# The sample sequences' SSM states in a two-layer hybrid decoder step: two alternating slots and masked sums, against unrolled quarters, three slots and column tiles

## Chip, core and metric

One core of a Trainium2 chip. The metric is the device time of one launch in microseconds: the median over the runs, smaller is better.

## What is computed

The kernel is one inference step of a decoder with an even layer (a depthwise convolution and latent attention) and an odd layer (Mamba-2 SSD), each followed by gated cross-attention. A prompt of 1024 tokens and 8 sample sequences of 4 tokens share the weights. The change touches one part of the odd layer: the carried state of the 8 sample sequences. For each sequence `b` there is a state of 32 heads x 64 x 128 numbers (1 MB in float32). From the reference, for one sequence's 4 tokens:

```python
y = y + jnp.einsum('btgn,bgepn->btgep', cf, state) * jnp.exp(cum)[..., None]
to_end = jnp.exp(cum[:, -1:] - cum) * dt
new_state = (state * jnp.exp(cum[:, -1])[..., None, None]
             + jnp.einsum('bsge,bsgn,bsgep->bgepn', to_end, bf, xf))
```

So the old state is read by the tokens' C vectors (the inter term, into YS), is scaled by a decay per head, and gets an update, a sum over 4 tokens of B times X; the new state is an output. The rest of `y` is computed later, in the chunks.

## The kernel before

The odd layer runs its stages one after the other, with a barrier of all engines between them: projections, then `ssd_all` (L2918), which loads small vectors, calls `sample_states` (L2966; the stage of this text), then `ssd_chunks` (L2623: 8 prompt chunks of 128 tokens and one chunk with the 32 sample tokens), then `store_state`. The order of the work on each engine is written out by hand, engine by engine, with semaphores.

**Data of the stage.** The state of a sequence lies as 128 partitions x 16 blocks (k) x 128, in `SB`, in two slots (sequence b in slot b % 2). `NW`, two slots, holds the new state until it is stored. All 8 PSUM banks are used: four named U and four named V, which change roles from one sequence to the next. XT holds the sample tokens' convolved x, B and C by channel, BT is B by token (32 x 512), XE is x by token scaled by to_end (32 x 2048), `bm` is a 0/1 mask of which of the 32 tokens belongs to sequence b. DE holds the decays. YS (32 x 2048) gathers the inter term.

**Head of the stage.** SyncE loads XT (L2986), eight small rows of ce (L2989) and the first two states (L2992). TensorE turns x and B of the tokens (L3019, L3021). VectorE copies BT (L3075), forms te (L3077), clears YS (L3078, 32 x 2048), and after ScalarE's exponential forms XE (L3082) and copies ce (L3086). Only then does TensorE begin with the states.

**One sequence (b).**
- TensorE: 16 transposes of the state (L3028) into the four banks of slot b; 4 matmuls of 128 x 32 by 128 x 512 (L3036), one per group, C against the turned state, each into the partitions 0 to 31 of a bank of the other side (all 32 tokens, of which 4 are of sequence b); 16 matmuls (L3041) with 32 rows that multiply the masked x by B, into the four banks from which the turned state has been copied; then the transposes of b + 1.
- ScalarE: copies the turned state from the four banks to SBT (L3067), one slot.
- VectorE: masks XE by sequence (XM, L3089, 32 x 2048), scales the state by the decay (L3091, 128 x 2048), adds the masked rows of the four banks to YS (L3097, four of 32 x 512), adds update and scaled state into NW (L3107, four of 128 x 512).
- SyncE: when VectorE is done with b - 2's state, it issues the load of state b (L2997), and for b = 2 to 5 one of four 2 MB parts of the output weights WO (L3001).
- GpSimd: issues the store of NW (L3011). VectorE waits for the store two sequences back (f_s) before it writes that NW slot.

These follow one another through semaphores: L3036 waits for all four copies (f_te) and the previous sequence's NW (f_un); the transposes of b + 1 wait for YS (f_yo). GpSimd waits for all stores at the end of the stage.

**The next stage.** `ssd_chunks` issues on SyncE's queue the loads of XT (L2662, 1.5 MB), CBt (L2666, 2 MB) and Z (L2670). TensorE's first instruction (L2713) waits for XT; VectorE's (L2841) for CBt. Before the first chunk's inter matmuls TensorE waits for WO (r_w 64, L2726), though WO is first used in `out` of chunk 0 (L2702), which runs in chunk 1.

Of the kernel before, what the change touches and what calls it, by code (L numbers as in the profile page):

```python
# [22 lines left out]
P = 128  # L23
# [105 lines left out]
def build(nc, A, O):  # L129
# [2493 lines left out]
    def ssd_chunks(W, DTt, CUt, ST, YS):  # L2623
# [6 lines left out]
        with ExitStack() as c:  # L2630
# [63 lines left out]
            def _(pe):  # L2694
                def out(n, T, halves=(0, 1)):

                    for hf in halves:
                        if hf == 0:

                            pe.wait_ge(r_ye, n * 4 + 4)  # L2700
                        for k in range(NX):
                            m = nc.tensor.matmul(OP[hf][0:T, :], YT[:, k, 0:T], WO[:, k, hf * 512:(hf + 1) * 512],  # L2702
                                                 start=k == 0, stop=k == NX - 1)
                        m.then_inc(r_om, 1)

                def chunk(n, T, sample, first):
# [206 lines left out]
    f_l = [sem(f"state_slot{k}") for k in range(2)]  # L2913
    f_s = [sem(f"state_stored{k}") for k in range(2)]
    f_tp, f_te, f_yi, f_yo, f_xm, f_up, f_un, f_out, f_c = (sem(n) for n in (
        "fs_tp", "fs_tp_out", "fs_inter", "fs_inter_out", "fs_xm", "fs_update", "fs_new", "fs_stored", "fs_x_loaded"))
# [23 lines left out]
    def store_state(ST):  # L2940

        with ExitStack() as c:
# [10 lines left out]
            @block.vector  # L2953
            def _(dve):
                dve.wait_ge(f_tp, NB + 2)
# [10 lines left out]
    def sample_states(DTt, CUt, DE, msk, bm, YS, WO):  # L2966

        with ExitStack() as c:
            XT = sb(c, "fXT", [P, XB, SMP])
            XE, BT = sb(c, "fXE", [SMP, SI]), sb(c, "fBT", [SMP, 4, SN])  # L2970
            XM = [sb(c, f"fXM{a}", [SMP, SI]) for a in range(2)]
            SB = [sb(c, f"fSB{a}", [P, NX, SN]) for a in range(2)]
            NW = [sb(c, f"fNW{a}", [P, NX, SN]) for a in range(2)]
            SBT = sb(c, "fSBT", [P, SI])
            ce, te = sb(c, "fce", [SMP, SH]), sb(c, "fte", [SMP, SH])
            U = [pb(c, f"fU{a}") for a in range(4)]
            V = [pb(c, f"fV{a}") for a in range(4)]
            BK = (U, V)
# [6 lines left out]
            def _(sp):  # L2985
                sp.dma_start(XT[:], xbc_d[:, :, TP:TOK].rearrange("n p t -> p n t")).then_inc(f_c, 16)  # L2986

# [6 lines left out]
                for b in range(2, NB):  # L2994

                    sp.wait_ge(f_un, 1 + b - 1)
                    sp.dma_start(SB[b % 2][:], s_in[b]).then_inc(f_l[b % 2], 16)  # L2997
                    if b < 6:

                        part = slice(4 * (b - 2), 4 * (b - 1))  # L3000
                        sp.dma_start(WO[:, part, :], w_out[:, part, :]).then_inc(r_w, 16)  # L3001

            @block.gpsimd
            def _(pool):

                for count in (f_yi, f_yo, f_up, f_un):
                    pool.nop().then_inc(count, 1)
                with loop(pool, 0, NB // 2) as j:
                    for s in range(2):
                        pool.wait_ge(f_un, 1 + 2 * j + s + 1)  # L3010
                        pool.dma_start(s_out[bass.ds(2 * j + s, 1)].rearrange("b p k n -> p (b k) n"), NW[s][:]).then_inc(f_s[s], 16)  # L3011
# [4 lines left out]
            def _(pe):  # L3016
                pe.wait_ge(f_c, 16 * (NB + 1))
                for k in range(NX):
                    nc.tensor.transpose(U[k // 4][0:SMP, (k % 4) * P:(k % 4 + 1) * P], XT[:, k, :], ident[:])  # L3019
                for g in range(4):  # L3020
                    t = nc.tensor.transpose(V[0][0:SMP, g * P:(g + 1) * P], XT[:, NX + g, :], ident[:])  # L3021
                t.then_inc(f_tp, 1)
                pe.wait_ge(dve_own.sem, d0 + 6)
                def turn(b, s, step):

                    pe.wait_ge(f_l[s], 16 * (step + 1))
                    for k in range(NX):
                        t = nc.tensor.transpose(BK[s][k // 4][:, (k % 4) * P:(k % 4 + 1) * P], SB[s][:, k, :], ident[:])  # L3028
                    t.then_inc(f_tp, 1)

                def batch(b, s, step, last=False):

                    pe.wait_ge(f_te, 4 * b + 4)
                    pe.wait_ge(f_un, 1 + b)
                    for g in range(4):
                        m = nc.tensor.matmul(BK[1 - s][g][0:SMP, :], XT[:, NX + 4 + g, :], SBT[:, g * 512:(g + 1) * 512],  # L3036
                                             start=True, stop=True)
                    m.then_inc(f_yi, 1)
                    pe.wait_ge(f_xm, b + 1)
                    for k in range(NX):  # L3040
                        m = nc.tensor.matmul(BK[s][k // 4][:, (k % 4) * P:(k % 4 + 1) * P], XM[s][:, k * P:(k + 1) * P],  # L3041
                                             BT[:, k // 4, :], start=True, stop=True)
                    m.then_inc(f_up, 1)
                    if not last:

                        pe.wait_ge(f_yo, 1 + b + 1)
                        turn(b + 1, 1 - s, step + s)

                turn(0, 0, 0)
                with loop(pe, 0, NB // 2 - 1) as j:  # L3050
                    for s in range(2):
                        batch(2 * j + s, s, j)
                batch(NB - 2, 0, NB // 2 - 1)
                batch(NB - 1, 1, NB // 2 - 1, True)

            @block.scalar
            def _(act):
                act.wait_ge(dve_own.sem, d0 + 3)
                nc.scalar.activation(te[:], te[:], ACT.Exp).then_inc(act_own.sem, 1)
                with loop(act, 0, NB // 2) as j:  # L3060
                    for s in range(2):
                        b = 2 * j + s
                        act.wait_ge(f_tp, b + 2)

                        act.wait_ge(f_yi, 1 + b)
                        for g in range(4):
                            nc.scalar.activation(SBT[:, g * 512:(g + 1) * 512], BK[s][g][:], ACT.Copy).then_inc(f_te, 1)  # L3067

# [3 lines left out]
            def _(dve):  # L3072
                v, N = (lambda ins: dve_own.step(dve, ins)), nc.vector
                dve.wait_ge(f_tp, 1)
                v(N.tensor_copy(BT[:], V[0][0:SMP, :].rearrange("p (g n) -> p g n", g=4)))  # L3075
                dve.wait_ge(f_c, 16 * (NB + 1))
                v(N.tensor_tensor(te[:], ce[:], CUt[0:SMP, NQ, :], ALU.subtract))  # L3077
                v(N.memset(YS[:], 0.0))  # L3078
                dve.wait_ge(act_own.sem, a0 + 1)
                v(N.tensor_tensor(te[:], te[:], DTt[0:SMP, NQ, :], ALU.mult))  # L3080
                for g in range(4):
                    dve_own_ins = N.tensor_tensor(XE[:, g * 512:(g + 1) * 512].rearrange("p (h e) -> p h e", e=SP_),  # L3082
                                                  U[g][0:SMP, :].rearrange("p (h e) -> p h e", e=SP_),
                                                  te[:, g * 8:(g + 1) * 8].unsqueeze(2).to_broadcast([SMP, 8, SP_]), ALU.mult)
                v(dve_own_ins)
                v(N.tensor_copy(ce[:], te[:]))  # L3086
                def ready(b, s):

                    N.tensor_scalar(XM[s][:], XE[:], bm[:, bass.ds(b, 1)], None, ALU.mult).then_inc(f_xm, 1)  # L3089
                    dve.wait_ge(f_tp, b + 2)  # L3090
                    v(N.tensor_tensor(SB[s][:], SB[s][:], DE[:, :, bass.ds(b, 1)].to_broadcast([P, NX, SN]), ALU.mult))  # L3091

                def batch(b, s, step, last=False):
                    dve.wait_ge(f_yi, 1 + b + 1)
                    for g in range(4):
                        part = YS[:, g * 512:(g + 1) * 512]
                        ins = N.scalar_tensor_tensor(out=part, in0=BK[1 - s][g][0:SMP, :], scalar=bm[:, bass.ds(b, 1)],  # L3097
                                                     in1=part, op0=ALU.mult, op1=ALU.add)
                    ins.then_inc(f_yo, 1)
                    dve.wait_ge(f_yo, 1 + b + 1)  # L3100
                    dve.wait_ge(f_up, 1 + b + 1)
                    if not (isinstance(step, int) and step == 0):

                        dve.wait_ge(f_s[s], 16 * step)
                    for g in range(4):
                        part = slice(4 * g, 4 * g + 4)
                        ins = N.tensor_tensor(NW[s][:, part, :], SB[s][:, part, :],  # L3107
                                              BK[s][g][:].rearrange("p (k n) -> p k n", k=4), ALU.add)
                    ins.then_inc(f_un, 1)
                    if not last:  # L3110
                        ready(b + 1, 1 - s)

                ready(0, 0)
                batch(0, 0, 0)
                batch(1, 1, 0)
                with loop(dve, 1, NB // 2 - 1) as j:
                    dve_own.enter(j - 1, 2)
                    for s in range(2):
# [40 lines left out]
```

## Time and profile of the kernel before

| what | us |
|---|---|
| median of 3 runs | 3184.64 (3182.26 to 3197.51) |
| the profiled execution, own time | 3189.32 |
| its span in the profile | 3187.7 |
| `sample_states`, from the first load's issue (L2986) to the next stage's first issue (L2662) | 2013.25 to 2147.17: 133.9 |
| one sequence in the middle of it | 13.1 |

The profile is one execution taken by the hardware profiler. PE is TensorE's matmuls, PEld its weight loads, DVE is VectorE, ACT ScalarE, POOL GpSimd, SPq and POOLq the queues on which SyncE and GpSimd issue transfers. Times are in microseconds from the start of the span. Over the whole span TensorE is busy 88%, VectorE 47%, ScalarE 24%, GpSimd 16%. PEclk is the clock that TensorE was granted, as a share of full speed. A float32 matmul shows as two records, a transpose as one. In a timeline row, what stands in brackets is the engine's idle time before it and what ended it.

### The profile page before, as it was taken

To read this page: it belongs to the slowest core of one execution; us is meant where nothing else is said; L and a number is where in the kernel's file an instruction comes from. 1 tells how busy PE (TensorE), PEld (TensorE's weight loads), DVE (VectorE), ACT (ScalarE), POOL (GpSimd) and SP (SyncE) were. 2 spreads that over 40 slices of the span, in tenths; PEclk is the share of its full clock that TensorE was granted. 3 is DMA by queue.
4 is the path that set the end of the run, shared out by engine and by line. 5 is a ranking of instruction groups with operands and counts; after the bars stand their busy time and mean duration, and the time that the engine had idled before them with its cause. 6 is when DMAs were issued, how large, how long until landed. Compare 5 with 4: busy or idle time off the path is not lost. (4 is left out here: it accounts for less than half of the span.)

```text
span 3187.7 us, 40235 instructions
## 1 busy us (share of the span) xinstructions
PE 2791.4 (88%) x16311; PEld 2213.6 (69%) x16311; DVE 1485.6 (47%) x2481; ACT 767.1 (24%) x1451; POOL 520.1 (16%) x422
## 2 busy tenths in 40 slices
PE   5999896897978999898998699667999995899889
PEld 4998564675856997778998477445555543599676
DVE  4997664564321005445655400356777733100453
ACT  3221353232211212323222211112222111121231
POOL 1012000341301210121221010002121211121011
PEclk9999898997988998998999899787999897899999
DMA  3211001761031114203221221464332303211431
GB/s 98 60 38 45 14 1 70 277 241 61 1 119 53 47 56 170 80 1 85 87 92 62 80 95 47 137 209 118 108 99 79 74 1 114 65 47 40 168 110 48
DMA packets 235495, 270.70 MB, mean 85 GB/s; under 512 B 36358, under 2 KB 190534, under 8 KB 230099
## 3 DMA queue, kind: packets, MB, share of 16 engines
q1 hardware_dynamic: 215506, 179.83, 18.9%
q0 software_dynamic: 16384, 75.77, 6.6%
q10 hardware_dynamic: 3456, 12.98, 1.0%
q8 instruction: 110, 1.80, 0.2%
q14 instruction: 39, 0.32, 0.0%
HBM read 226.64 MB, written 41.28 MB: 84 GB/s over the span
## 5 line engine op out<-in xcount | busy, mean ns | idle before, releaser
L306 PE MATMUL pp<-HH,WS_part 128*128 128x352 f32 x1776 | 574.9, 324 | 0.0
L304 PE MATMUL pp<-HH,WH 128*128 128x352 f32 x1344 | 436.9, 325 | 40.1 <-POOL WS_part L443 40.1
L305 PE MATMUL pp<-HT_part,WH 128*128 128x352 f32 x1344 | 435.0, 324 | 0.0
L306 PEld LDWEIGHTS pp<-HH,WS_part 128*128 128x128 f32 x1776 | 337.2, 190 | 0.0
L304 PEld LDWEIGHTS pp<-HH,WH 128*128 128x128 f32 x1344 | 254.8, 190 | 42.1 <-POOL WS_part L443 42.1
L2702 PE MATMUL OP<-oWO,YT 128*128 128x512 f32 (+1 forms) x576 | 255.8, 603 | 3.3 <-DVE XE L2829 3.3
L305 PEld LDWEIGHTS pp<-HT_part,WH 128*128 128x128 f32 x1344 | 254.9, 190 | 0.0
L2161 DVE COPY HT<-zT 128x512 f32<-128x512 f32 x64 | 44.2, 691 | 437.1 <-DMA xown<-c_batch 383.6
L443 POOL TENSOR_TENSOR WS_part<-WS,WH 128x1024 fp32r<-128x1024 f32 x56 | 140.4, 2507 | 655.0 <-ACT WH L394 655.0
L2702 PEld LDWEIGHTS OP<-oWO,YT 128*128 128x128 f32 (+1 forms) x576 | 104.8, 183 | 146.4 <-issue 142.9
L998 DVE SCALAR_TENSOR_TENSOR CV<-GXP,cw,CV 128x512 f32<-128x512 f32 x240 | 161.9, 739 | 0.0
L304 PE MATMUL pp<-HH,CK_part 128*128 128x352 f32 x432 | 142.0, 329 | 7.9 <-DVE HT_part L863 7.9
L305 PE MATMUL pp<-HT_part,CK_part 128*128 128x352 f32 x432 | 140.5, 325 | 0.0
L304 PE MATMUL zp<-WZH,HH 128*128 128x512 f32 (+1 forms) x288 | 114.6, 398 | 14.7 <-ACT ZS L2540 14.0
L304 PE MATMUL yp<-QT_part,KM_part 128*128 128x512 f32 (+1 forms) x288 | 115.0, 399 | 13.2 <-DVE WO_part L606 13.2
L306 PE MATMUL yp<-QT_part,SGX_part 128*128 128x512 f32 (+1 forms) x288 | 114.8, 399 | 0.0
L305 PE MATMUL yp<-WO_part,KM_part 128*128 128x512 f32 (+1 forms) x288 | 114.7, 398 | 0.0
L306 PE MATMUL zp<-WZH,HT_part 128*128 128x512 f32 (+1 forms) x288 | 113.8, 395 | 0.0
L305 PE MATMUL zp<-WZ_part,HH 128*128 128x512 f32 (+1 forms) x288 | 113.5, 394 | 0.0
L2683 POOL TENSOR_TENSOR XK<-XK,Db 128x2048 f32<-128x2048 f32 (+1 forms) x9 | 88.1, 9786 | 136.8 <-DVE XD L2855 136.8
L2382 DVE SCALAR_TENSOR_TENSOR oACC<-EP,cwo,oACC 128x1024 f32<-128x1024 f32 x72 | 98.7, 1370 | 9.2 <-DVE oACC L2380 2.4
L1732 DVE COPY QN<-KTp 128x512 f32<-128x512 f32 x128 | 82.7, 686 | 27.6 <-PE KTp L1658 27.6
(493 smaller groups left out, 5224.6 us busy)
## 6 DMA issues: line engine op xcount, KB each, us to landing
WS<-x_w_qg SPq DMA_DIRECT2D x32, 512.0 KB, 4.0
WO<-cache_mem_k SPq DMA_DIRECT2D x16, 1024.0 KB, 4.9
WO<-cache_mem_v POOLq DMA_DIRECT2D x16, 1024.0 KB, 5.4
CBt<-cum_scratch SPq DMA_DIRECT2D x8, 2048.0 KB, 10.1
xbc_scratch<-oACC ACTq DMA_DIRECT2D x24, 528.0 KB, 2.7
WS<-o_w_in SPq DMA_DIRECT2D x24, 512.0 KB, 3.7
XT<-xbc_scratch SPq DMA_DIRECT2D x8, 1536.0 KB, 7.5
WS<-e_w_in SPq DMA_DIRECT2D x18, 512.0 KB, 3.9
```

The lines of the kernel that those rows point to most:

```text
L304: nc.tensor.matmul(out, wh, xh, start=start, stop=False)
L305: nc.tensor.matmul(out, wh, xl, start=False, stop=False)
L306: return nc.tensor.matmul(out, wl, xh, start=False, stop=stop)
L443: nc.gpsimd.tensor_tensor(WL[:, k % slots, :, :], WS[:, k % slots, :, :], WH[k % 2][:, :, :], ALU.subtract).then_inc(p_lo, 1)
L998: ins = nc.vector.scalar_tensor_tensor(out=out, in0=src, scalar=tap, in1=out, op0=ALU.mult, op1=ALU.add)
L1732: nc.vector.tensor_copy(KTs[:, r, :], KTp[r % 3][:]).then_inc(d_kte, 1)
L2161: nc.vector.tensor_copy(KBT[b % 2][:, 2 * q:2 * q + 2, :], KTp[:].rearrange("p (k m) -> p k m", k=2))\
L2382: ins = nc.vector.scalar_tensor_tensor(out=out, in0=src, scalar=tap, in1=out, op0=ALU.mult, op1=ALU.add)
L2683: nc.gpsimd.tensor_tensor(XK[R, :].rearrange("p (h e) -> p h e", h=SH), XK[R, :].rearrange("p (h e) -> p h e", h=SH), Db[R, :].unsqueeze(2 ...
L2702: m = nc.tensor.matmul(OP[hf][0:T, :], YT[:, k, 0:T], WO[:, k, hf * 512:(hf + 1) * 512], start=k == 0, stop=k == NX - 1)
```

## The change

The loop over sequences is unrolled on every engine. Each sequence is cut in quarters of 4 blocks. PSUM is divided anew: three banks for turned quarters (TPp), four for updates (UP), one (ACC) for the inter term. The state gets three slots, SBT two. TensorE's order becomes: for each quarter q, transposes of quarter q of b + 1 (`turn`), update matmuls of quarter q of b (`update`), and after quarter 0 the inter matmuls of b (`inter`). In `inter` the four groups go to four column tiles, partitions 32g to 32g + 31 of one bank, which keeps summing over all 8 sequences; the C operand CMB is masked so that other tokens add zero. The mask for the update moves from x (32 x 2048) to B (BM, 32 x 512). VectorE forms the new state in one operation per block, state x decay + update (16 of 128 x 128), with no separate scaling pass and no YS sums. After the last sequence ACC is copied, and four matmuls with column slices of the identity bring the four partition groups to partitions 0 to 31, from where they are copied to YS. The four WO parts are issued after all state loads, and the wait for them moves from the first chunk to `out`.

```diff
@@ ssd_chunks, TensorE: out, chunk
                             pe.wait_ge(r_ye, n * 4 + 4)
+                            pe.wait_ge(r_w, 64)
...
-                    if first:
-                        pe.wait_ge(r_w, 64)
-                    else:
+                    if not first:
@@ sample_states, SyncE
-                for s in range(2):
-                    sp.dma_start(SB[s][:], s_in[s]).then_inc(f_l[s], 16)
+                for b in range(NB):
+                    if b >= 3:
+                        sp.wait_ge(f_un, 4 * (b - 2))
+                    sp.dma_start(SB[b % 3][:], s_in[b]).then_inc(f_l[b % 3], 16)
...
+                for a in range(4):
+                    sp.dma_start(WO[:, 4 * a:4 * a + 4, :], w_out[:, 4 * a:4 * a + 4, :]).then_inc(r_w, 16)
@@ GpSimd
+                for b in range(NB):
+                    pool.wait_ge(f_un, 4 * (b + 1))
+                    pool.dma_start(s_out[b], NW[b % 2][:]).then_inc(f_s[b % 2], 16)
@@ TensorE
+                def turn(b, q):
+                    if q == 0:
+                        pe.wait_ge(f_l[b % 3], 16 * (b // 3 + 1))
+                    i = 4 * b + q
+                    if i >= 3:
+                        pe.wait_ge(f_te, i - 2)
+                    for k in range(4):
+                        t = nc.tensor.transpose(TPp[i % 3][:, k * P:(k + 1) * P], SB[b % 3][:, 4 * q + k, :], ident[:])
+                    t.then_inc(f_tp, 1)
+                def inter(b):
+                    pe.wait_ge(f_te, 4 * b + 4)
+                    for g in range(4):
+                        m = nc.tensor.matmul(ACC[32 * g:32 * g + 32, :], CMB[:, g, b, :], SBT[b % 2][:, g * 512:(g + 1) * 512],
+                                             start=b == 0, stop=b == NB - 1, tile_position=(0, 32 * g), skip_group_check=True)
+                    m.then_inc(f_yi, 1)
+                def update(b, q):
+                    if q == 0:
+                        pe.wait_ge(f_xm, b + 1)
+                    i = 4 * b + q
+                    if i >= 4:
+                        pe.wait_ge(f_un, i - 3)
+                    for k in range(4):
+                        m = nc.tensor.matmul(UP[q][:, k * P:(k + 1) * P], XE[:, (4 * q + k) * P:(4 * q + k + 1) * P],
+                                             BM[b % 2][:, q, :], start=True, stop=True)
+                    m.then_inc(f_up, 1)
...
+                for q in range(4):
+                    turn(0, q)
+                pe.wait_ge(dve_own.sem, d0 + 7)
+                for b in range(NB):
+                    for q in range(4):
+                        if b + 1 < NB:
+                            turn(b + 1, q)
+                        update(b, q)
+                        if q == 0:
+                            inter(b)
+                pe.wait_ge(f_un, 4 * NB + 1)
+                for g in range(4):
+                    m = nc.tensor.matmul(UP[g][0:SMP, :], ident[:, 32 * g:32 * g + 32], YA[:], start=True, stop=True)
+                m.then_inc(f_up, 1)
@@ ScalarE
+                        nc.scalar.activation(SBT[b % 2][:, q * 512:(q + 1) * 512], TPp[i % 3][:], ACT.Copy).then_inc(f_te, 1)
@@ VectorE
+                v(N.memset(CMB[:], 0.0))
...
+                for b in range(NB):
+                    ins = N.tensor_copy(CMB[:, :, b, TS * b:TS * b + TS], XT[:, NX + 4:NX + 8, TS * b:TS * b + TS])
...
-                v(N.memset(YS[:], 0.0))
...
+                def masked(b):
+                    if b >= 2:
+                        dve.wait_ge(f_up, 4 * (b - 1))
+                    N.tensor_scalar(BM[b % 2][:], BT[:], bm[:, b:b + 1], None, ALU.mult).then_inc(f_xm, 1)
...
+                for b in range(NB):
+                    if b + 1 < NB:
+                        masked(b + 1)
+                    if b >= 2:
+                        dve.wait_ge(f_s[b % 2], 16 * (b // 2))
+                    for q in range(4):
+                        dve.wait_ge(f_up, 4 * b + q + 1)
+                        for k in range(4 * q, 4 * q + 4):
+                            ins = N.scalar_tensor_tensor(out=NW[b % 2][:, k, :], in0=SB[b % 3][:, k, :], scalar=DE[:, k, b:b + 1],
+                                                         in1=UP[q][:, (k - 4 * q) * P:(k - 4 * q + 1) * P], op0=ALU.mult, op1=ALU.add)
+                        ins.then_inc(f_un, 1)
+                dve.wait_ge(f_yi, NB)
+                N.tensor_copy(YA[:], ACC[:]).then_inc(f_un, 1)
+                dve.wait_ge(f_up, 4 * NB + 1)
+                for g in range(4):
+                    ins = N.tensor_copy(YS[:, g * 512:(g + 1) * 512], UP[g][0:SMP, :])
+                v(ins)
```

## Rows read from the trace of the kernel before

**Rows 1.** The windows view, first two rounds; columns on its first line.
```profile
core 0: us, PE busy (x) PEld busy (x) DVE busy (x) ACT busy (x) POOL busy (x), PEclk, DMA share, GB/s
2030.70:2045.40 14.70, 12.33 (x57) 7.99 (x57) 6.28 (x6) 2.07 (x4) 0.00 (x0) 0.70 0.01 1
2045.40:2058.50 13.10, 10.95 (x57) 6.39 (x56) 8.58 (x10) 2.06 (x4) 1.24 (x1) 0.87 0.68 228
```

**Rows 2.** The timeline, stage's start and second round: start, us, engine, line, what.
```profile
2018.62 2.76 SPq L2992 DMA_DIRECT2D fSB<-state_ssm  x2
...
2025.67 1.76 DVE L3078 MEMSET YS<- 32x2048 f32 x1 [0.48 <-DVE fte L3077]
...
2030.75 3.68 PE L3028 MATMUL fU<-ident,fSB 128*128 128x128 f32 x16 [6.49 <-DVE fce L3086]
...
2047.37 2.06 ACT L3067 ACTIVATE fSBT<-fV 128x512 f32<-128x512 f32 x4 [10.76 <-PE fV L3028]
...
2048.10 0.69 SPq L2997 DMA_DIRECT2D fSB<-state_ssm  x1
...
2049.49 5.32 PE L3036 MATMUL fU<-fSBT,fXT 128*32 128x512 f32 x8 [2.15 <-ACT fSBT L3067]
...
2054.74 3.64 PEld L3041 LDWEIGHTS fV<-fBT,fXM 32*128 32x128 f32 x32 [0.84 <-issue]
2054.74 3.83 PE L3041 MATMUL fV<-fBT,fXM 32*128 32x128 f32 x32
2054.92 2.71 DVE L3097 SCALAR_TENSOR_TENSOR YS<-fU,bm,YS 32x512 f32<-32x512 f32 x4 [3.50 <-PE fU L3036]
...
2058.50 1.96 PE L3028 MATMUL fU<-ident,fSB 128*128 128x128 f32 x16
2058.68 2.48 DVE L3107 TENSOR_TENSOR fNW<-fSB,fV 128x512 f32<-128x512 f32 x4 [1.05 <-PE fV L3041]
```

**Rows 3.** The timeline at the stage's end and the next's start.
```profile
2137.01 2.48 DVE L3107 TENSOR_TENSOR fNW<-fSB,fV 128x512 f32<-128x512 f32 x4 [1.90 <-issue]
2140.41 1.15 POOL L3011 DMA_DIRECT2D out<-fNW  x1 [12.96 <-DVE fNW L3107]
2147.17 0.37 SPq L2662 DMA_DIRECT2D XT<-xbc_scratch  x1
...
2154.77 3.67 PE L2713 MATMUL V<-ident,XT 128*128 128x128 f32 x16 [17.85 <-DMA XT<-xbc_scratch]
...
2162.00 0.20 DVE L2841 COPY dc<-CBt 128x32 f32<-128x32 f32 x1 [14.41 <-DMA CBt<-cum_scratch]
```

**Rows 4.** The groups by line and form on VectorE: mean ns of one.
```profile
L878 DVE SCALAR_TENSOR_TENSOR CKV<-pe,krs,X_part 128x128 f32<-128x128 f32 x8 | 2.8, 346 | 1.8 <-POOL krs L1012 1.8
...
L2324 DVE COPY HC<-ohp 128x24 f32<-128x24 f32 x24 | 2.2, 171 | 9.7 <-PE ohp L2312 9.7
```

**Rows 5.** The timeline on TensorE, even layer's sample attention, scores in column tiles.
```profile
640.77 1.04 PE L1671 MATMUL Sc<-QN,DTt_part 128*32 128x512 f32 x8
641.75 1.53 PE L1658 MATMUL KTp<-ident,HT 128*128 128x128 f32 x12
```

**Rows 6.** The timeline on TensorE, the round where L3036 ran at full clock.
```profile
2089.20 3.62 PE L3036 MATMUL fV<-fSBT,fXT 128*32 128x512 f32 x8 [2.31 <-ACT fSBT L3067]
```

**Rows 7.** The instructions of tile fSB: landing times of its loads.
```profile
DMA to landing us min/median/max: 6.3/6.5/8.6
```

**Rows 8.** The DMA view, window 2048 to 2060: two queues, one landing.
```profile
q1 hardware_dynamic: 899, 2.57, 63.4%
q0 software_dynamic: 272, 1.05, 23.1%
...
out<-fNW POOLq DMA_DIRECT2D x1, 1024.0 KB, 10.0
```

**Rows 9.** The DMA view, window 2018 to 2030, the row of queue q1.
```profile
q1 hardware_dynamic: 1458, 2.10, 66.0%
```

**Rows 10.** The DMA view, window 2126 to 2138, the row of queue q0.
```profile
q0 software_dynamic: 272, 1.05, 30.1%
```

More of the change, by code:

```diff
@@ L2912, in build @@
     r_seg = sem("ssd_seg_ready")
[L2913 removed]
+    f_l = [sem(f"state_slot{k}") for k in range(3)]
     f_s = [sem(f"state_stored{k}") for k in range(2)]
[L2915 to L2916 removed]
+    f_xt, f_tp, f_te, f_yi, f_xm, f_up, f_un, f_out, f_c = (sem(n) for n in (
+        "fs_x_tp", "fs_tp", "fs_tp_out", "fs_inter", "fs_masked", "fs_update", "fs_new", "fs_stored", "fs_x_loaded"))
     def ssd_all(DTt, CUt, DE):
@@ L2968, in sample_states @@
         with ExitStack() as c:
-            XT = sb(c, "fXT", [P, XB, SMP])
+            XT, CMB = sb(c, "fXT", [P, XB, SMP]), sb(c, "fCMB", [P, 4, NB, SMP])
             XE, BT = sb(c, "fXE", [SMP, SI]), sb(c, "fBT", [SMP, 4, SN])
-            XM = [sb(c, f"fXM{a}", [SMP, SI]) for a in range(2)]
-            SB = [sb(c, f"fSB{a}", [P, NX, SN]) for a in range(2)]
+            BM = [sb(c, f"fBM{a}", [SMP, 4, SN]) for a in range(2)]
+            SB = [sb(c, f"fSB{a}", [P, NX, SN]) for a in range(3)]
             NW = [sb(c, f"fNW{a}", [P, NX, SN]) for a in range(2)]
[L2974 to L2978, printed above, removed]
+            SBT = [sb(c, f"fSBT{a}", [P, SI]) for a in range(2)]
+            ce, te, YA = sb(c, "fce", [SMP, SH]), sb(c, "fte", [SMP, SH]), sb(c, "fYA", [P, 512])
+            TPp = [pb(c, f"fTP{a}") for a in range(3)]
+            UP = [pb(c, f"fUP{a}") for a in range(4)]
+            ACC = pb(c, "fACC")
             s_in = A["state_ssm"][0].rearrange("b (k a) p n -> b (a p) k n", a=2)
@@ L3024, in turn @@
[L3024 to L3054, printed above, removed]
+                    t = nc.tensor.transpose(ACC[0:SMP, g * P:(g + 1) * P], XT[:, NX + g, :], ident[:])
+                t.then_inc(f_xt, 1)
+                for q in range(4):
+                    turn(0, q)
+                pe.wait_ge(dve_own.sem, d0 + 7)
@@ L3056, in _ @@
             @block.scalar
             def _(act):
-                act.wait_ge(dve_own.sem, d0 + 3)
+                act.wait_ge(dve_own.sem, d0 + 4)
                 nc.scalar.activation(te[:], te[:], ACT.Exp).then_inc(act_own.sem, 1)
[L3060 to L3067, printed above, removed]
+                for b in range(NB):
+                    for q in range(4):
+                        i = 4 * b + q
+                        act.wait_ge(f_tp, i + 1)
+                        if q == 0 and b >= 2:
+                            act.wait_ge(f_yi, b - 1)
+                        nc.scalar.activation(SBT[b % 2][:, q * 512:(q + 1) * 512], TPp[i % 3][:], ACT.Copy).then_inc(f_te, 1)
@@ L3086, in _ @@
+                v(ins)
                 v(N.tensor_copy(ce[:], te[:]))
[L3087 to L3118, printed above, removed]
-                        batch(2 * j + s, s, j)
-                    dve_own.leave(NB // 2 - 2)
-                batch(NB - 2, 0, NB // 2 - 1)
-                batch(NB - 1, 1, NB // 2 - 1, True)
+                def masked(b):
+                    if b >= 2:
+                        dve.wait_ge(f_up, 4 * (b - 1))
+                    N.tensor_scalar(BM[b % 2][:], BT[:], bm[:, b:b + 1], None, ALU.mult).then_inc(f_xm, 1)
@@ new lines, in _ @@
+                masked(0)
+                for b in range(NB):
+                    if b + 1 < NB:
+                        masked(b + 1)
+                    if b >= 2:
+                        dve.wait_ge(f_s[b % 2], 16 * (b // 2))
+                    for q in range(4):
+                        dve.wait_ge(f_up, 4 * b + q + 1)
[3 more added lines that the diff above has]
+                        ins.then_inc(f_un, 1)
```

31 lines of the change are left out of this document (8 added, 23 removed).

## The prediction

> **What bounds the kernel now.** I read the windows view over the stage first [rows 1]. A round, one sample sequence, takes 13.1 us, and in it no engine is full: TensorE 10.95, VectorE 8.58, ScalarE 2.06. So the round is a chain of waits. The timeline shows it [rows 2]: transposes of the next state (1.96 us), ScalarE's copies (2.06) with TensorE idle 2.15 before the inter matmuls, these (5.32), the update matmuls (3.83), and transposes again. VectorE's sums and additions hang beside it. The sum 1.96 + 2.15 + 5.32 + 3.83 is 13.3, less small overlaps the 13.1. Eight rounds and a head and tail make the stage's 133.9 us, and a barrier stands at either end. At its end [rows 3] VectorE finishes at 2139.5, the last store is issued at 2140.41, and the next stage issues its load of XT at 2147.17. TensorE starts there when XT lands (2154.77), VectorE when CBt does (2162.00). What follows is untouched, so the whole change is worth what those two landings move.
>
> **The change, part by part.** I lay out a new timeline against the profiled execution (3189.32 us, span 3187.7); that one lies 4.7 us, 0.15%, above the median, so I subtract the same gain from 3184.64.
>
> *VectorE.* Scaling, masked x and YS sums go. Per sequence there are 16 operations of 128 x 128 with a PSUM operand. The nearest row has 346 ns for one [rows 4]; four of 32 x 512 of the same operation end in 2.71 us, so one starts before the other ends by about 0.07, and I take 0.276 each: 4.4 us, plus a mask of 32 x 512 at about 0.4. That is 4.8 us in place of 8.58, off the path. Its last quarter ends about 1.2 us after TensorE's.
>
> *TensorE.* Transposes as before, 16 for 1.97 less the pipeline's end: 1.8. Updates as before: 3.8. The inter matmuls in four column tiles: the same form stands in the even layer, where eight records of 128 x 512 take 1.04 us and the next group starts 0.98 after them [rows 5], against 3.62 us one behind the other at full clock [rows 6] and 5.32 with a clock that fell. I take 1.0. The work is 6.6 us. The Trainium skill, page "TensorE: Matmul & The Clock Gate", section "Measured speedup vs the span model", has 2.38 times for three column tiles; by that the inter part would be some 1.5 us and a round 0.5 longer. Row 640.77 is this form with four tiles and gives 3.5 times, so I go by the row.
>
> *Switches between forms.* The new order mixes 128-row transposes, 32-row updates and column tiles: nine switches per sequence where there were three. From updates to transposes the matmuls go on without a gap (3.83 from 2054.74, next at 2058.50) [rows 2]; before a switch to updates the weight loads stand still for 0.84. Neither is the cost in the new order: the lower bound is 0, the upper 0.84. A drained pipeline must pay the latency that a transpose shows beyond its slot, some 0.2 us (1.96 for 16 that start every 0.11), and that is the nearest: 9 x 0.2 = 1.8. So TensorE needs 8.4 us a round (6.6 with free switches, 14.2 with the dearest).
>
> *ScalarE* has the same 2.06 us in quarters [rows 2], with three banks ahead of it: hidden behind TensorE's updates; without that cover up to 2.15 us a round come back.
>
> *The load loop.* SyncE waits for VectorE's end of b - 3, issues 0.1 to 0.2 us later, and the state lands 6.3 to 8.6, median 6.5 us, after the issue [rows 7]. TensorE wants it one own round later. So a round can't be under 1.2 + 0.2 + 6.5 + 0.1 = 8.0 us, or 10.1 with a landing of 8.6. *The store loop.* VectorE waits for the store of b - 2: about 1 us to issue, 10.0 to land beside WO [rows 8], then its own 4.8; two rounds hold this if one is 7.9. *Transfers.* A load of 1.05 MB costs half of 66.0% of 12 us, 4.0 us of the DMA engines [rows 9]; a store 23.1% of 12, 2.8, to 30.1% of 12, 3.6 [rows 8, 10]: 6.8 to 7.6 a round. All these lie just under 8.4; I take **8.4 us a round**, 4.7 less than now.
>
> *Head.* The YS memset (1.76 us) leaves VectorE's chain [rows 2]; eight copies of at most 0.17 each come in [rows 4], the CMB memset runs while it waits. The start at 2030.75 becomes about 2030.1. The first state's transposes (3.68 us at half clock) move into the wait, as the first load, issued at 2018.62, lands after 6.3 or a little more, near 2025. Round 0 began with a granted clock of 0.70 [rows 1]; I give it 11.5 us, between 8.4 and about 15.
>
> *Sum.* Round 0 ends at 2041.6, six rounds of 8.4 at 2092.0, round 7, without transposes, at 2097.1, VectorE's last state at 2098.3. New tail: copy of ACC 0.7, four matmuls one behind the other 5.3 (3.6 at full clock), four copies to YS 2.5 (as L3107): 2107. The last store, issued at 2099.3 and landing in 10.0 us instead of 6.1, ends at 2109.3; it decides. Next stage's issue: 0.6 later, **2109.9** against 2147.17.
>
> *What is late next: WO.* Its four parts, 8.4 MB, are now issued behind the last state load, when VectorE ends sequence 4 (2041.6 + 33.6 + 1.2 = 2076.4), on the queue that carries XT, CBt and Z afterwards. In window 2048 to 2060 q1 moves 2.57 MB in 63.4% of 12, 7.6 us; less the state's 4.0, 1.52 MB of WO take 3.6, so 8.4 MB take 20 us. With one load (4.0) and four stores (11.2 to 14.4) that is 35 to 38 us from about 2077.5 on: until some 2114.5. XT's 1.5 MB come behind it; alone it lands 7.6 us after its issue, some 5.5 of it transfer. XT then lands near **2120**, not 2117.5, and CBt, on the same queue, keeps its distance. Gain: 2154.8 - 2120, about 35 us. The wait for WO, moved to `out`, is met long before and costs nothing. Predicted: 3184.6 - 35 = **3150 us**; the profiled time would be 3154.
>
> **Rivals.**
> 1. *Forecast*, 0.72: rounds of 7.6 to 9.5 us. The lower end, a clock that rises at once and no WO ahead of XT give 3140; the upper 3156.
> 2. *The load loop rules*, 0.08: landings of 8.6 as the longest one, a round of 10.1. Stage end 2109.9 + 6 x 1.7 = 2120, XT 2127.7: gain 27, 3158. For it: each load now runs beside a store from the start; against: the loads already do so in rows 7, and land in 6.5.
> 3. *The change doesn't do what it says*: the column tiles run one behind the other, 0.08. The inter part is then 3.6 us, the round 11.0, the stage's end 2128, XT at 2135.7: gain 19, 3166. Against it stands row 640.77.
> 4. *The clock stays at its lower level*, 0.08, because TensorE keeps stopping in small waits. Twice the 6.6 and 1.8 for switches: 15 us a round. The stage's end moves to about 2158, XT to 2166: 11 us slower than now, 3196, within 0.5%. Against: in the second round the clock was 0.87 with 2.15 us of idle in it, and the new order has less idle.
> 5. *Slower: the switches*, 0.04. Each of nine costs the 0.84 that rows 2 show before L3041, and these stops hold the clock down: 13.2 + 7.6 = 21 us a round. Stage end near 2200, XT 2208: 54 us slower, 3238. It decides from 13.4 us a round on, and is slower by 0.5% from 15.5. The Trainium skill, page "TensorEngine Tiling (Array Packing)", section "Key Properties", speaks for it: a change of tiling mode drains the engine. The trace agrees that something stands still (0.84), but the updates' first matmul starts at 2054.74, before the inter matmuls' last one ends (2049.49 + 5.32), so TensorE itself loses little there.
>
> **Numbers.** A measurement of this kernel can tell some 0.5%, 16 us, from no change. Faster by more: cases 1, 2, 3, 0.88. Within: case 4, 0.08. Slower: 0.04. The range 3135 to 3168 holds cases 1 to 3 with the bounds of the switches (free ones make 8.0 the round, the load loop's; 10.5 makes 3160).
>
> **What would show it.** Right: rounds of 8 to 9 us between first transposes of successive states, TensorE over 85% busy in them and PEclk near 1; inter groups of about 1 us; VectorE idle a third of a round; load landings near 6.5; the next stage's XT issued at about 2110 and landing over 8 us later, with WO still moving. Wrong: rounds over 11 us; a PEclk of 0.5 to 0.7 in the middle rounds; VectorE waiting for a store (f_s); inter groups of 3.6 us; or XT landing in 7.6 us, which would say that WO is out of the way by then.

## The result

The median of the changed kernel is 3168.72 us against 3189.55 before, in nine runs each. One run of the nine took 6950.69 us and is set aside as disturbed; the median of the other eight is 3167.96. The ratio without it is 0.9946, 95% interval 0.9923 to 0.997. The two medians lie 21 us apart, the ratio stands for 17: about 0.5 to 0.7%, where 35 us were forecast, and at the upper end of the range (3135 to 3168). The others spread from 3161.60 to 3187.01 where the kernel before spreads from 3182.26 to 3197.51. The profiled execution took 3163.62 us.

The windows view of the changed kernel, over five of its rounds (columns in its first line):

```profile
core 0: us, PE busy (x) PEld busy (x) DVE busy (x) ACT busy (x) POOL busy (x), PEclk, DMA share, GB/s
2025.20:2032.90 7.70, 7.70 (x57) 5.71 (x57) 4.20 (x14) 2.50 (x5) 0.00 (x0) 1.00 0.27 77
2032.90:2040.60 7.70, 7.70 (x57) 5.66 (x56) 4.87 (x17) 2.39 (x4) 1.21 (x1) 1.00 0.61 173
2041.60:2055.70 14.10, 14.10 (x58) 10.19 (x57) 4.90 (x18) 2.39 (x4) 1.15 (x1) 0.50 0.57 177
2055.70:2069.70 14.00, 14.00 (x57) 10.14 (x56) 4.82 (x18) 2.39 (x4) 1.15 (x1) 0.50 0.49 150
2092.40:2100.00 7.60, 7.60 (x57) 5.64 (x56) 4.79 (x18) 2.39 (x4) 1.15 (x1) 1.00 1.02 411
```

These answer to [rows 1]. A round now takes 7.7 us at a granted clock of 1.00 and 14.1 at 0.50, the lower of TensorE's two levels (1.2 and 2.4 GHz). TensorE is busy all through in both. The clock was at the upper level for two rounds, at the lower from 2041 to 2089, and up again after that.

The timeline of the changed kernel on TensorE, where the clock falls (start, duration, what; the idle time before and its releaser in brackets):

```profile
2038.88 0.66 PE L3016 MATMUL fTP<-ident,fSB 128*128 128x128 f32 x4
...
2041.03 0.66 PE L3016 MATMUL fTP<-ident,fSB 128*128 128x128 f32 x4 [0.41 <-DMA fSB<-state_ssm]
...
2041.62 2.07 PE L3034 MATMUL fUP<-fBM,fXE 32*128 32x128 f32 x8
...
2043.62 1.94 PE L3022 MATMUL fACC<-fSBT,fCMB 128*32 128x512 f32 x8
```

Up to 2041 TensorE has not stopped for 15 us. Then it waits 0.41 us for the load of the fourth state, and the next group already runs at half speed (2.07 in place of 1.15, then 1.94 in place of 1.07). The timeline at the stage's end answers to [rows 3]:

```profile
2106.05 4.22 DVE L3111 SCALAR_TENSOR_TENSOR fNW<-fSB,DE,fUP 128x128 f32<-128x128 f32 x16 [3.71 <-DMA out<-fNW]
2110.19 0.68 DVE L3115 COPY fYA<-fACC 128x512 f32<-128x512 f32 x1
2110.83 1.15 POOL L3002 DMA_DIRECT2D out<-fNW  x1 [7.04 <-DVE fNW L3111]
...
2117.42 2.47 DVE L3118 COPY YS<-fUP 32x512 f32<-32x512 f32 x4 [6.54 <-PE fUP L3057]
2121.93 0.37 SPq L2662 DMA_DIRECT2D XT<-xbc_scratch  x1
...
2129.81 3.67 PE L2714 MATMUL V<-ident,XT 128*128 128x128 f32 x16 [12.44 <-DMA XT<-xbc_scratch]
...
2137.05 0.19 DVE L2840 COPY dc<-CBt 128x32 f32<-128x32 f32 x1 [14.69 <-DMA CBt<-cum_scratch]
```

The stage's first load is issued at 2009.19 here, so it takes 112.7 us against 133.9: 21.2 us less, as much as the medians differ. (This profile reached the stage 4 us earlier than the one before, which the change has no part in. In all 16 profiles of this text, what lies outside the stage takes 3042 to 3060 us. So a stage is compared more sharply than a total, and a few us of a median are not assigned to a cause.) XT lands 7.9 us after its issue (7.6 before), so WO hardly delayed it. But VectorE waits 3.71 us for a store at the last state.

### The profile page after: what moved, and what is told of

The parts are those of the page before. It is cut to its first block and busy times, and to the rows that moved or that the text cites. A ratio compares the mean times of both kernels' runs of the same rounds, so it can differ in the third digit from the quotient of the medians.

```text
span 3161.8 us, 40215 instructions
## 1 busy us (share of the span) xinstructions
PE 2785.7 (88%) x16319; PEld 2218.8 (70%) x16319; DVE 1458.5 (46%) x2550; ACT 769.3 (24%) x1451; POOL 518.9 (16%) x422
```

## The experiments

The theories after this result: A, this mix of transposes and of matmuls that fill 32 rows or 32 columns doesn't hold the upper clock; B, the wait for a load lets it fall. "Stage" is from the first load's issue to the next stage's first issue, in each run's profile; ratios are to the kernel before, measured beside each run (its medians are 3181 to 3192 us).

**The changed kernel again**, twice (no edit).

> The changed kernel again, for a second look at when TensorE's granted clock falls. In its first profile rounds took 7.7 us while the clock was at its upper level (first two and last rounds) and 14.06 us in between, at the lower level. Theory A (the mix of transposes and of matmuls that fill only 32 rows or 32 columns of the array does not count for much, so the clock falls although TensorE never stops): it falls again, at much the same place, and 3 to 4 rounds take 14 us; stage 105 to 115 us, 15 to 28 us faster than the kernel before. Theory B (the wait of 0.4 us for the load of the fourth state, at 2041, lets the clock fall): it falls wherever a load is waited for, so the place and the length can differ from the first profile.

> The changed kernel once more, for its spread on this chip beside the others, and a third profile of the clock. Theory C (a stop with 32-row updates lets the clock fall): some runs stop and fall, at the first load waited for, and the time then depends on how long the clock stays down: a spread of 20 us and more between runs, where four slots spread over 6. In the profile the fall comes right behind a wait for a load.

Measured: 3162.98 us (four runs, 3145.77 to 3174.88), ratio 0.9891 (0.9847 to 0.9934), stage 120.0; and 3169.25 us (twelve runs, 3149.35 to 3183.11 without one disturbed), ratio 0.9929 (0.9902 to 0.9957), stage 114.6. TensorE's timeline of the first:

```profile
2036.76 1.15 PE L3034 MATMUL fUP<-fBM,fXE 32*128 32x128 f32 x8
2038.09 0.66 PE L3016 MATMUL fTP<-ident,fSB 128*128 128x128 f32 x4 [0.18 <-DMA fSB<-state_ssm]
2038.68 1.65 PE L3034 MATMUL fUP<-fBM,fXE 32*128 32x128 f32 x8
2040.26 1.94 PE L3022 MATMUL fACC<-fSBT,fCMB 128*32 128x512 f32 x8
```

and of the second:

```profile
2038.36 1.15 PE L3034 MATMUL fUP<-fBM,fXE 32*128 32x128 f32 x8
2039.82 0.66 PE L3016 MATMUL fTP<-ident,fSB 128*128 128x128 f32 x4 [0.31 <-DMA fSB<-state_ssm]
2040.41 2.01 PE L3034 MATMUL fUP<-fBM,fXE 32*128 32x128 f32 x8
```

In all three profiles the clock falls at the first wait for a load, after two rounds of 7.7 us: 0.41, 0.18 and 0.31 us of waiting. It stayed down for 3.4, over 5 and 4.4 rounds; the stages of 112.7, 120.0 and 114.6 us follow that order. The first of these expectations gave A 105 to 115, which 120.0 misses.

**No later loads.** `for b in range(NB)` becomes `for b in range(3)` in SyncE's loads, and `turn` waits for `f_l[b % 3], 16`; loads 4 to 8 are left out. WO is still issued when VectorE ends the fifth sequence (`sp.wait_ge(f_un, 20)`).

> Only the first three states are loaded, and the slots are used again for the others; so loads 4 to 8 are left out of the computation, and TensorE never waits for one after the first rounds. Theory A: the clock falls all the same, and rounds of 14 us appear; stage 105 to 115 us, as the changed kernel. Theory B: no wait, so the clock stays at the upper level, rounds of 7.7 us to the end (the store loop may make them 8); stage about 91 us, some 43 us faster than the kernel before.

Measured: 3144.15 us, ratio 0.9844 (0.9818 to 0.9869); stage 91.2. Two windows:

```profile
2060.00:2076.00 16.00, 16.00 (x120) 12.02 (x119) 8.26 (x30) 4.91 (x9) 2.30 (x2) 1.00 0.81 294
2076.00:2085.00 9.00, 8.21 (x40) 6.05 (x38) 6.35 (x25) 0.00 (x0) 1.15 (x1) 0.54 1.02 409
```

From 2022 to 2076, seven rounds of 7.7, the clock is at 1.00. That is B's number, and A is out for these rounds: the same mix held the clock for 54 us. It isn't out for the last round, which has no transposes. There the clock falls at about 2076.6 with no stop before it, and the inter matmuls with the last twelve update matmuls take 7.4 us, where they take 3.9 in the first profile of the changed kernel, at the upper clock. The same fall without a stop stands in the last round of five more profiles with 32-row updates below (fourth slot, one column tile, one stop with 32 rows, WO late, first turn late).

**Updates over 128 rows.**

```diff
-            XE, BT = sb(c, "fXE", [SMP, SI]), sb(c, "fBT", [SMP, 4, SN])
-            BM = [sb(c, f"fBM{a}", [SMP, 4, SN]) for a in range(2)]
+            XE, BT = sb(c, "fXE", [P, SI]), sb(c, "fBT", [SMP, 4, SN])
+            BM = [sb(c, f"fBM{a}", [P, 4, SN]) for a in range(2)]
...
+                N.memset(XE[:], 0.0)
+                N.memset(BM[0][:], 0.0)
+                v(N.memset(BM[1][:], 0.0))
```

> The update matmuls take 128 rows instead of 32, of which 96 are zeros in both operands; nothing else changes, and at the same clock they should take the same time. Theory A: with whole rows in the updates the clock holds; rounds of about 7.7 us (8.0 where a load is waited for), stage about 91 to 94 us, some 40 us faster than the kernel before and 20 faster than the changed one. If zeros do not count as activity, it falls as before. Theory B: the loads are waited for as before, the clock falls as before, stage 105 to 115 us.

Measured: 3141.23 us, ratio 0.9828 (0.9809 to 0.9847); stage 89.7. Its timeline on TensorE:

```profile
2037.57 1.06 PE L3034 MATMUL fUP<-fBM,fXE 128*128 128x128 f32 x8
2038.46 0.60 PE L3016 MATMUL fTP<-ident,fSB 128*128 128x128 f32 x4
2038.90 1.06 PE L3034 MATMUL fUP<-fBM,fXE 128*128 128x128 f32 x8
2041.52 0.66 PE L3016 MATMUL fTP<-ident,fSB 128*128 128x128 f32 x4 [1.57 <-DMA fSB<-state_ssm]
2042.02 1.06 PE L3034 MATMUL fUP<-fBM,fXE 128*128 128x128 f32 x8
2043.00 1.07 PE L3022 MATMUL fACC<-fSBT,fCMB 128*32 128x512 f32 x8
```

Now TensorE stops for 1.57 us, longer than in any round of the changed kernel, and goes on at full speed. So B alone is out too. It holds through stops of 1.10 and 2.25 us as well, but not through the last one:

```profile
2070.63 1.06 PE L3034 MATMUL fUP<-fBM,fXE 128*128 128x128 f32 x8
2073.92 1.11 PE L3016 MATMUL fTP<-ident,fSB 128*128 128x128 f32 x4 [2.23 <-DMA fSB<-state_ssm]
2074.83 1.92 PE L3034 MATMUL fUP<-fBM,fXE 128*128 128x128 f32 x8
2077.93 0.66 PE L3016 MATMUL fTP<-ident,fSB 128*128 128x128 f32 x4
```

Behind 2.23 us the clock is at its lower level too, but by 2078 it is up again. With 128 rows a stop can let the clock fall; what is different is that it is back within about 4 us. The run also prices the switches: a quarter starts every 1.33 us in place of 1.67, and the two switches in it are what went, 0.17 us each. Rounds still average 7.8 us, since loads (7.2 us in all) and stores (12.9) are waited for.

**Transposes as plain matmuls.** `nc.tensor.transpose(..., ident[:])` becomes `nc.tensor.matmul(..., ident[:], start=True, stop=True)` in `turn`.

> The transposes of the states become plain float32 matmuls against the identity, two records each: 1.9 us more TensorE work a round at the upper clock, 3.8 at the lower. Theory A, if it is the transposes that do not count: the clock holds, rounds of 9.6 us, no wait for loads, stage about 103 us, 9 us faster than the changed kernel. Theory A, if it is the 32-row updates: the clock falls, rounds of 17 to 18 us, slower than the changed kernel by 10 us or more. Theory B: rounds of 9.6 leave no wait for a load, so the clock holds too.

Measured: 3159.51 us, ratio 0.9912 (0.9876 to 0.9947); stage 102.8, rounds of 9.7, no load waited for, clock 1.00. It stands with B, and with theory C, which the later expectations use: a stop lets the clock fall, and with 32-row updates it stays down for rounds.

**A fourth slot**, in ST's memory: `SB = [...three...] + [ST as 16 blocks]`, `b % 4`, load b waits for `f_un, 4 * (b - 3)`, and GpSimd clears ST behind the last transposes.

> The changed kernel with a fourth state slot (in the memory of ST, which is cleared again behind the stage), so that every load has two rounds instead of one and TensorE has no load to wait for; all loads and stores are made. After the first four runs theory C is: a stop of TensorE is what lets the clock fall, and with 32-row updates it does not come back for four to five rounds; without a stop, or with whole rows, it holds. Theory C: rounds of 7.7 to 7.9 us throughout, stage 90 to 93 us, 3140 to 3150 us in total. Rival D (the clock held without the loads because the transfers were gone, not the wait): it falls, stage 110 to 120 us.

Measured: 3140.21 us (3137.45 to 3143.28), ratio 0.9861 (0.9834 to 0.9888); stage 90.4. Two of its windows:

```profile
2021.00:2029.00 8.00, 8.00 (x60) 5.93 (x59) 4.42 (x16) 2.51 (x5) 0.00 (x0) 1.00 0.68 188
...
2061.00:2069.00 8.00, 8.00 (x64) 5.70 (x56) 4.70 (x17) 2.39 (x4) 1.47 (x2) 1.00 1.02 408
```

All transfers are made, up to 408 GB/s, and the clock holds until the last round: it was the wait, not the traffic. Rival D (the transfers) is out.

**One column tile**: `inter` writes `ACC[0:32, :]` for all four groups without `tile_position`; the inter term is not separated by group. VectorE clears ACC first.

> The four inter matmuls of a sequence all go to the first column tile, one behind the other, into partitions 0 to 31 of the bank (so the inter term is summed over groups and is not separated; that part of the result is left out). This prices the column tiles and makes a round longer than a load. At the upper clock the inter part takes 3.6 us instead of 1.07, a round 10.3. Theory C: no load is waited for, the clock holds, seven rounds of 10.3, stage 108 to 111 us: no slower than the changed kernel in its usual state (113 and 120 us). Rival (the clock falls by itself with these forms): rounds of 19 us, stage over 140 us.

Measured: 3161.45 us, ratio 0.9929 (0.9901 to 0.9956); stage 109.9, rounds of 10.2, the inter part 3.62 us. Column tiles save 2.55 us a round, 19 in the stage (91.2 with three loads). But the changed kernel, which has them, is no faster (112.7 to 120.0): the shorter round is what makes TensorE wait for a load. At the head of this run stands a stop with 32-row updates that cost little:

```profile
2021.13 0.66 PE L3016 MATMUL fTP<-ident,fSB 128*128 128x128 f32 x4 [1.11 <-DVE fce L3094]
2022.80 5.32 PE L3022 MATMUL fACC<-fSBT,fCMB 128*32 128x512 f32 x8
```

The inter matmuls take 5.32 us in place of 3.62, the clock is 0.50 from 2024 to 2026, and 1.00 from 2028 on.

**One stop added** (TensorE waits until VectorE has ended the second state) to the kernel with three loads, with 32 and with 128 rows: `if q == 0 and b == 3: pe.wait_ge(f_un, 8)` in `turn`.

> The kernel with only three loads (loads 4 to 8 left out), in which the clock held, with one stop added: before the transposes of the fourth state TensorE waits until VectorE has finished the second one, about 1.2 us. Theory C: the clock falls behind this one stop and stays at its lower level for several rounds of 14 us; stage 110 to 120 us. Rival D: one stop costs 1.2 us and no more, stage about 92 to 93 us.

> The run with one added stop of 1.3 us (three loads only; loads 4 to 8 left out), now with updates over 128 rows. Theory C: the same stop, but the clock holds, as it held through stops of 1 to 2 us with 128 rows and all loads; stage 82 to 88 us. Rival (it was the place of the stop, not the form of the work): the clock falls as it did with 32 rows, stage 100 us or more.

With 32 rows, TensorE's timeline:

```profile
2035.91 1.15 PE L3034 MATMUL fUP<-fBM,fXE 32*128 32x128 f32 x8
2038.33 0.81 PE L3016 MATMUL fTP<-ident,fSB 128*128 128x128 f32 x4 [1.26 <-issue]
2039.06 2.07 PE L3034 MATMUL fUP<-fBM,fXE 32*128 32x128 f32 x8
2041.06 1.94 PE L3022 MATMUL fACC<-fSBT,fCMB 128*32 128x512 f32 x8
```

and with 128:

```profile
2029.38 1.06 PE L3034 MATMUL fUP<-fBM,fXE 128*128 128x128 f32 x8
2031.70 0.63 PE L3016 MATMUL fTP<-ident,fSB 128*128 128x128 f32 x4 [1.26 <-issue]
2032.16 1.06 PE L3034 MATMUL fUP<-fBM,fXE 128*128 128x128 f32 x8
2033.15 1.06 PE L3022 MATMUL fACC<-fSBT,fCMB 128*32 128x512 f32 x8
```

The same stop of 1.26 us costs 16.3 us of stage in the one (107.5 against 91.2; 3151.82 us in total, 3138.93 to 3153.98) and no fall behind it in the other (stage 85.8; 3132.42 us, 3129.16 to 3134.84). The first was expected at 110 to 120. This is the plainest pair for C: the stop with 32-row updates is followed by 34 us at the lower level. (Its fastest run, 3138.93 us, has no profile; whether the clock was down as long there isn't known.) The run with 128 rows shows more:

```profile
2017.16 0.66 PE L3016 MATMUL fTP<-ident,fSB 128*128 128x128 f32 x4 [1.86 <-DVE fce L3096]
2066.65 1.48 PE L3034 MATMUL fUP<-fBM,fXE 128*128 128x128 f32 x8 [2.43 <-DVE fNW L3114]
```

The clock held through the first of these; behind the second it was at 0.50 from 2068 to 2070, and at 1.00 by 2072.

**Better versions.** Both parts; then the tail of the inter term on ScalarE and in the free transpose banks; then WO issued behind the next stage's first loads; then all four. Last, four slots with `turn(0, q)` put behind the wait for ce.

> Updates over 128 rows (96 of zeros) and the fourth slot together. TensorE's own work was 6.5 us a round in the run with 128 rows, which waited 7.2 us in total for loads and had VectorE wait 12.9 us for stores. Without the load waits: the store loop (10 us to land, 1 to issue, 4.6 of VectorE, in two rounds) gives 7.8 us a round, so about the same stage as with three slots, 88 to 90 us; if the stores land sooner than that, 82 to 86. Total 3130 to 3142 us.

> Four slots as before, and the end of the inter term moved: ScalarE copies the bank of sums as soon as the last inter matmuls are done, TensorE turns it into the free transpose banks, ScalarE writes YS; VectorE has no part in it. With four slots alone this tail lay behind VectorE's last state: copy 0.7, matmuls 5.7, copies 2.5, and the next stage's first issue came at 10.9 us behind that last state (2083.8 to 2094.7). Theory: then the last store decides, some 10 us after VectorE's end too (10.3 landing and 0.6 to issue), so the gain is 0 to 1 us: no difference that a measurement shows against four slots alone; stage 89 to 91 us, total 3138 to 3145. Rival (the tail decides): stage 84 to 86.

> As the one before, with the four WO loads issued behind the first chunk's loads of the next stage instead of inside this one. My forecast had WO delay the stores and XT. Theory: without WO beside them the last stores land in 6 to 7 us instead of 10.3, VectorE stops waiting for them, and the stage ends 4 to 8 us earlier (82 to 86 us); XT lands 7.6 us after its issue; WO is needed only about 45 us later, so nothing is paid for it. Total some 5 us below the kernel before it in this list. Rival: the stores are slow because of the state loads beside them, and the stage keeps its length.

> Updates over 128 rows, four slots, the early tail and the late WO together. With four slots and 32 rows (the two kernels with the early tail) the runs still spread over 40 and 50 us, and their profiles show a stop of 1.86 us at the head of the stage, behind the first state's transposes, in which the clock, already risen, fell. Theory C: with 128 rows no such stop lets it fall, so the spread is under 15 us and the median the lowest of all that give the whole result, 3128 to 3138; stage 82 to 87 us. Rival: the spread comes from elsewhere in the kernel and stays at 40 us.

> Four slots with 32 rows (the run that held its clock), with the first state's transposes put behind the wait for ce, as in the kernel before, so that no stop lies between them and the first round. It starts with its transposes 3.7 us later at the lower clock. Theory C: no stop anywhere in the rounds, so all runs hold the clock: median 3142 to 3148, spread under 15 us, stage 92 to 95 us. Rival: the clock also falls without a stop in some runs: spread of 30 us or more.

| kernel | updates' rows | slots | median, us (runs) | lowest to highest | ratio, 95% | stage |
|---|---|---|---|---|---|---|
| both parts | 128 | 4 | 3139.20 (4) | 3128.69 to 3147.75 | 0.9809 to 0.9879 | 87.7 |
| early tail | 32 | 4 | 3140.14 (6) | 3132.20 to 3173.07 | 0.9819 to 0.9905 | 110.5 |
| and WO late | 32 | 4 | 3143.26 (6) | 3128.41 to 3178.32 | 0.9827 to 0.9897 | 88.0 |
| all four | 128 | 4 | 3127.09 (5) | 3124.34 to 3136.88 | 0.9797 to 0.9841 | 77.9 |
| first turn late | 32 | 4 | 3141.37 (5) | 3136.29 to 3145.45 | 0.9844 to 0.9891 | 93.4 |

The two with the early tail and 32 rows missed their expectation: they spread by 41 and 50 us, and the stages are 110.5 (89 to 91 expected) and 88.0 (82 to 86). In the first one's timeline the fall stands at the head of the stage:

```profile
2011.48 0.66 PE L3019 MATMUL fTP<-ident,fSB 128*128 128x128 f32 x4 [0.37 <-ACT fSBT L3074]
2014.00 0.66 PE L3019 MATMUL fTP<-ident,fSB 128*128 128x128 f32 x4 [1.86 <-DVE fce L3102]
2014.58 1.15 PE L3037 MATMUL fUP<-fBM,fXE 32*128 32x128 f32 x8
2015.67 1.31 PE L3025 MATMUL fACC<-fSBT,fCMB 128*32 128x512 f32 x8
```

Here the clock had risen under the first transposes (0.66 for four, where the other runs have 1.1), and the wait for ce, 1.86 us, became a stop at the upper level; from 2016 to 2020 the clock is 0.54 in the mean, and three rounds took 13.4 to 14.1. But the second one has the same stop, and the same 32 rows:

```profile
2022.86 0.66 PE L3020 MATMUL fTP<-ident,fSB 128*128 128x128 f32 x4 [1.86 <-DVE fce L3103]
2024.75 1.94 PE L3026 MATMUL fACC<-fSBT,fCMB 128*32 128x512 f32 x8
2027.66 1.15 PE L3038 MATMUL fUP<-fBM,fXE 32*128 32x128 f32 x8
```

There the clock falls too, but is up again before 2028. So C doesn't say how long the clock stays down, and nothing here shows what decides it. With the first transposes behind that wait (last row) the spread is 9 us, but that kernel has the old tail, and with the old tail and the old head the fourth slot alone spread by 6: the last row doesn't show that the head made the difference. With all four parts the spread is 13.

WO late left the first four stores, beside the state loads, as slow as ever (9.2 to 10.0 us to land) and took the last four from 10.1 to 10.9 us (WO beside them) to 6.0. In the kernel with all four, VectorE ends at 2079.4, and the next stage issues at 2086.71, the last store landed. Median and stage are better than expected (3128 to 3138, 82 to 87). Its ratio, 0.9819, is the lowest of all that give the whole result, 54 us below the kernel before (3181.39 beside it), but its interval overlaps that of 128 rows alone (0.9828, 0.9809 to 0.9847); what shows the gain over that one is the stage, 77.9 against 89.7. How much of it is the late WO and how much the tail was not separated. The fourth slot adds little to the 128 rows (87.7 against 89.7), as VectorE then waits 16.2 us in all for stores.

## Why the prediction was wrong

- **The bound** and the way in which the gain comes were right: the two landings moved with the stage's end and nothing after it changed.
- **VectorE**: 16 operations in 4.2 us (forecast 4.4). It was off the path but for the last state, where the store two sequences back landed only 11.1 us after its issue, beside WO. VectorE ended 4.3 us behind TensorE there, not 1.2: the store loop, taken for harmless at 7.9 us a round, cost 3 us.
- **Inter in column tiles**: 1.07 us (forecast 1.0), by the row of the even layer [rows 5]. The Trainium skill's 2.38 times for three tiles ("TensorE: Matmul & The Clock Gate", section "Measured speedup vs the span model") was the worse guide: 3.62 against 1.07 is 3.4 times for four.
- **Switches**: 0.17 us for one (forecast 0.2). The round is 7.7 us at the upper clock, not 8.4: without switches it would be 6.3 (four quarters of 1.33 and 1.0 for the inter matmuls; forecast 6.6), so that the nine make 1.4 (forecast 1.8). Rival 5 is out, as its price of 0.84 is five times what was measured. By the Trainium skill's rule on mode changes ("TensorEngine Tiling (Array Packing)", section "Key Properties") the engine drains at one; the 0.17 us agree that something is paid.
- **The load loop**: landings of 6.7 us (median; 6.5 forecast), TensorE waits 0.2 to 0.4 us at the fourth state, a round of about 8. The forecast had this number, 8.0, and took it for harmless as it lay under 8.4.
- **The failed step** is "six rounds of 8.4": it takes the upper clock for granted. Behind the first wait for a load the clock was at its lower level for about 3.4 rounds of 14.06 us in the profile, and this is 3.4 x 6.4 = 22 us lost. The six rounds of 7.7 in place of 8.4 gave 4 of it back, round 0 another 4, the head 1; the store at the last state took 3. That makes 16, and the stage was forecast at 96.7 us and measured 112.7 (120.0 and 114.6 in the other two profiles). Rival 4, priced at 15 us a round for all rounds and given 0.08, named the mechanism, but not its trigger, and spoke against itself with "the new order has less idle": less idle did not help, as a single short stop was enough.
- **Head**: round 0 took 7.7 us, not 11.5: the clock rose at about 2024.7, at the end of the first state's transposes, which had been moved ahead.
- **Tail**: 11.7 us from VectorE's last state to the next issue, 11.6 forecast; the last store decides, as forecast (10.4 us to land). But the path by the sum's end is only 1.3 us shorter, as its four matmuls took 6.4 us at the lower clock, not 5.3.
- **WO behind the states**: the 2.5 us of delay for XT were put in and did not come: XT landed 7.9 us after its issue. Nor did they come in the kernels with a fourth slot and WO in the stage (7.6 and 7.9), which issue WO earlier. Only in the run with three slots and 128 rows, where WO was still moving when XT was issued, did XT take 9.1 us. What WO did delay were the stores (10.4 to 11.1 us beside it).

## What to carry to other kernels

When a change makes TensorE's rounds shorter, look for the first wait that it will newly meet, and price the clock behind that wait, not only the wait: here waits of 0.2 to 0.4 us were followed by 48 to 77 us at the lower level, which by the rounds of 14.06 and 7.7 us is 22 to 35 us lost. A round of nearly continuous work with 32-row matmuls in it is the fragile case here. One more buffer took the stops away; zero rows up to 128, at the same duration, let the clock hold through most stops and come back soon after the others. A wide spread between runs of one kernel can be a sign of it (34 us in the changed kernel, 6 with a fourth slot), but it isn't proof. The kernel before spread by 25 us beside that run, one far slower run left out. The kernel with 128 rows and four slots spread by 19, and its slowest run, which is the profiled one, held its clock through all rounds.

## What the runs showed that I had not expected

With 32-row updates, a stop of 0.18 us (the shortest seen) was followed by the lower clock for five rounds, though TensorE was busy without a gap in all of them; with 128-row updates, zeros in 96 of the rows, stops of 1.26, 1.57 and 1.86 us were not. And the last round, updates without transposes, lost the clock without any stop in six profiles with 32 rows (in four others it held) and in none with 128.

A stop with 32-row updates doesn't always cost rounds. The head stops of two runs above (one column tile, WO late) were followed by 3 to 4 us at the lower level, and the kernel before shows the same in its rounds, where TensorE stops 2.15 us and the updates have 32 rows too:

```profile
2049.50:2052.00 2.50, 2.50 (x4) 0.54 (x5) 1.91 (x1) 0.00 (x0) 0.48 (x1) 0.53 0.85 230
2054.80:2058.50 3.70, 3.70 (x33) 3.58 (x32) 2.71 (x4) 0.00 (x0) 0.00 (x0) 1.00 1.02 403
```

Its clock is at the lower level right behind the stop and back before the updates begin. What the chip measures was not tried and stays open. The lower level ended by itself at different times (after 3.4 rounds in one profile, 2.4 behind the added stop, over five in another), for which no run here shows a cause.
